# Attention with a woven S5 scan on one core: scores issued behind the second turn of a pair, maxima first on VectorE

## The reference

```python
q, k, v, u = split(h @ w_mix_in)                  # 512 columns each
# attention: 8 heads of 64; for branches (128,1), (512,4), (2048,16)
#   s = q.k * 64**-0.5 - slope_h * distance, masked; softmax; the branches
#   are mixed by their softmax denominators
# S5: 32 groups of 16 channels, 64 complex states each
bu = einsum(u, b_bar); states = scan(a_bar, bu); y = real(einsum(states, c)) + d*u
mixed = concat([attn, ssm]) @ w_mix_out
```

## Time and profile before

| | us |
|---|---|
| median of three runs | 3159.32 |
| lowest, highest | 3157.42, 3162.17 |
| profiled execution | 3157.16 |
| its span | 3155.3 |
| TensorE busy | 3036.2 (96%) |
| VectorE busy | 1376.3 (44%) |
| ScalarE busy | 869.7 (28%) |
| granted TensorE clock, mean | 0.989 |

### The profile page before, as it was taken

One profiled execution on the slowest core, in us unless ns is written; L12 is line 12 of the kernel. 1 busy time (PEld: TensorE's weight loads), 2 busy tenths in 40 slices (PEclk: granted clock), 3 DMA queues, 4 the chain that ended last, 5 costly groups with the idle time before them and its releaser, 6 DMA issues. The chain is left out here.

```text
span 3155.3 us, 36156 instructions
## 1 busy us (share of the span) xinstructions
PE 3036.2 (96%) x13904; PEld 2470.5 (78%) x13904; DVE 1376.3 (44%) x1715; ACT 869.7 (28%) x1313; POOL 411.8 (13%) x1004
## 2 busy tenths in 40 slices
PE   7999999999998989999999999999998999999998
PEld 5767888888886768888888877876677888888886
DVE  5653444444446353433343354335546333333336
ACT  6523211222113252111211133135644211121112
POOL 0001000000000000788870010011100000000000
PEclk9999999999999999999999999999999999999999
DMA  3112111111112022122221132212122111111113
GB/s 125 40 61 80 61 43 44 53 53 53 40 41 67 27 74 67 65 80 87 94 97 40 47 114 87 82 60 71 56 91 105 65 41 47 47 60 47 40 47 127
DMA packets 54405, 206.93 MB, mean 66 GB/s; under 512 B 7216, under 2 KB 7984, under 8 KB 52000
## 3 DMA queue, kind: packets, MB, share of 16 engines
q1 hardware_dynamic: 38592, 140.53, 13.3%
q0 software_dynamic: 15712, 65.02, 5.6%
HBM read 173.15 MB, written 31.20 MB: 65 GB/s over the span
## 5 line engine op out<-in xcount | busy, mean ns | idle before, releaser
L126 PE MATMUL ps<-region_a,region_b 128*128 128x512 f32 x1664 | 658.0, 395 | 18.1 <-DVE region_a L221 9.8
L128 PE MATMUL ps<-region_a,region_b 128*128 128x512 f32 x1664 | 649.9, 391 | 0.0
L127 PE MATMUL ps<-region_a,region_b 128*128 128x512 f32 x1664 | 649.8, 391 | 0.0
L815 DVE TENSOR_TENSOR acc<-acc,ps 128x1024 f32<-128x1024 f32 x288 | 350.9, 1219 | 332.2 <-PE ps L128 332.2
L126 PE MATMUL ps<-region_b,region_a 128*128 128x512 f32 x1088 | 432.6, 398 | 17.3 <-DVE region_b L121 10.0
L127 PE MATMUL ps<-region_b,region_a 128*128 128x512 f32 x1088 | 428.8, 394 | 0.0
L128 PE MATMUL ps<-region_b,region_a 128*128 128x512 f32 x1088 | 428.6, 394 | 0.0
L121 DVE TENSOR_TENSOR region_b<-raw,region_b 128x1024 fp32r<-128x1024 f32 x176 | 218.0, 1254 | 395.3 <-ACT region_b L117 395.1
L126 PEld LDWEIGHTS ps<-region_a,region_b 128*128 128x128 f32 x1664 | 314.2, 189 | 86.3 <-DVE region_b L121 7.3
L128 PEld LDWEIGHTS ps<-region_a,region_b 128*128 128x128 f32 x1664 | 313.7, 189 | 65.8
L127 PEld LDWEIGHTS ps<-region_a,region_b 128*128 128x128 f32 x1664 | 314.2, 189 | 64.8 <-issue 1.7
(11 more groups left out here) (290 smaller groups left out, 3204.5 us busy)
## 6 DMA issues: line engine op xcount, KB each, us to landing
raw<-stream SPq DMA_DIRECT2D x252, 512.0 KB, 3.3
ssm_row<-ssm_mid POOLq DMA_DIRECT2D x8, 1632.0 KB, 7.7
x_mid<-acc POOLq DMA_DIRECT2D x24, 512.0 KB, 3.0
ssm_mid<-made_osc POOLq DMA_DIRECT2D x8, 1024.0 KB, 4.3
ssm_mid<-made_out POOLq DMA_DIRECT2D x8, 608.0 KB, 3.3
acc<-x SPq DMA_DIRECT2D x8, 512.0 KB, 8.2
rold<-x POOLq DMA_DIRECT2D x16, 256.0 KB, 3.4
old_a<-x_mid POOLq DMA_DIRECT2D x8, 512.0 KB, 7.2
```

What stands on the lines that cost most here:

```text
L126: nc.tensor.matmul(psum, lhs(0), rhs(0), start=first, stop=False)
L127: nc.tensor.matmul(psum, lhs(0), rhs(1), start=False, stop=False)
L128: return nc.tensor.matmul(psum, lhs(1), rhs(0), start=False, stop=last)
L815: nc.vector.tensor_tensor(acc[:, t, :], acc[:, t, :], src, ALU.add).then_inc(F.sem["de"], 1)
```

## The change

Three things, in `att_pe` and `att_dve` alone. On TensorE, scores of a pair of blocks go from in front of the turns of the even block n to behind the turns of the odd block n - 1 (`EARLY` holds all odd steps, so it is so for every pair but the one issued at n = 0), and `factors` goes behind the scan's step. On VectorE, the maximum of block n + 2 comes first in each step, then `inverses`, then `finish`. The bias rows for the next pair of heads are made at r = 7 and r = 8, one each, the second behind the finish. What is computed is the same, and no instruction is added or taken away.

```diff
--- before.py
+++ after.py
@@ -1680,7 +1680,8 @@
         ot_hi, ot_lo = sem("ot_hi"), sem("ot_lo")
         NA = N_HEADS * NT
         NQ = NA // 4
-        BIAS_AT = 5
+        BIAS_AT = (7, 8)
+        EARLY = (1, 3, 5, 7)
         TILE_ORDER = (0, 1, 4, 5, 2, 3, 6, 7)
         TURNED_AT = {6: 0, 4: 0, 2: 4 * S, 0: 4 * S}
 
@@ -1808,16 +1809,18 @@
                         ins.then_inc(at_pv, 1)
 
             for n in range(NA):
-                if n % 2 == 0 and n + 2 < NA:
+                if n % 2 == 0 and n + 2 < NA and (n == 0 or (n - 1) % NT not in EARLY):
                     scores_pair(pe, n // 2 + 1)
                 if n == 0:
                     pe.wait_ge(u_out, GT)
                 transposes(n)
-                if n % 4 == 0 and n:
-                    factors(n // 4 - 1)
+                if n % 2 and n + 3 < NA and n % NT in EARLY:
+                    scores_pair(pe, (n + 3) // 2)
                 if n == 0:
                     ssm_turn_pe(pe, 0, 0)
                 ssm_step_pe(pe, n)
+                if n % 4 == 0 and n:
+                    factors(n // 4 - 1)
                 if n >= 4:
                     values(n // 4 - 1, n % 4)
             factors(NQ - 1)
@@ -1876,16 +1879,18 @@
 
             made = {}
             for n in range(NA):
+                if n + 2 < NA:
+                    maximum(dve, n + 2, made.get(block_of(n + 2)[0], 0))
+                if n % 4 == 0 and n:
+                    inverses(n // 4 - 1)
                 if n % 4 == 0 and n >= 8:
                     finish(n // 4 - 2)
-                if n % 4 == 0 and n:
-                    inverses(n // 4 - 1)
-                if n + 2 < NA:
-                    maximum(dve, n + 2, made.get(block_of(n + 2)[0], 0))
-                h, i = block_of(n + 2)
-                if i == BIAS_AT and h + 2 < N_HEADS:
-                    dve.wait_ge(at_m, n + 3)
-                    made[h + 2] = head_bias(dve, h + 2)
+                pair, r = divmod(n, 2 * NT)
+                if r in BIAS_AT and 2 * pair + 2 < N_HEADS:
+                    if pair:
+                        dve.wait_ge(at_m, 2 * NT * pair)
+                    h = 2 * pair + 2 + BIAS_AT.index(r)
+                    made[h] = head_bias(dve, h)
                 ssm_step_dve(dve, n)
                 ssm_rest_dve(dve, n)
             finish(NQ - 2)
```

## The result

The changed kernel takes 3188.15 us (median of 4 runs, 3184.21 to 3191.80) against 3159.59 before (4 runs): ratio 1.0092, 95% interval 1.0079 to 1.0104. It is slower by 28.6 us. Its profiled execution took 3191.8 us, with a span of 3190.0. The two profiled executions differ by 34.6 us in all (3191.8 and 3157.16), so 3.6 us of that lie outside the stage, 3.3 of them behind it, where the order is the same. The part behind the stage took between 864.6 and 868.1 us in the fourteen profiled executions of this document, so I read the 3.6 us as scatter, and the loss as that of the stage that the prediction spoke of.

What follows compares the result with a forecast made beforehand. It took TensorE's queue to be the bound (busy 44.65 of 48.50 us a pair). From 3157.2 us, 23.5 us of waits and 5.5 us of clock gave 3186 us, range 3172 to 3197.

Steps and rivals of the forecast that it cites:

- (a): Bias rows moved to r7 and r8 (blocks r0 to r15 of a pair): 1.65 us wait goes, 0.45 us left.
- (b): At r4 and r12: factor turns newly wait 1.5 us for att_o, the finish being behind maximum and inverses.
- (c): Scores of r8, r9 at r5 newly wait 2.0 us for r7's maximum behind the scan; at r13, 1.6 us.
- (d): Scores at r3 and r11 wait for a maximum queued behind m1b: 0.4 and 0.85 us.
- (e): Turn at r7 waits 0.65 us (before 0.19) for r6's copy, queued on ScalarE; at r15 also 0.65.
- (f): Factor turns at r0 and r8 wait for the finish: 0.25 and 0.1 us (before 0.6 at r0).
- The sum of the waits: TensorE's waits in a new pair, 9.95 against 3.85 us: +6.1 us a pair, +23.5 us over the stage.
- The clock: TensorE's granted clock falls in four surely idle places, 1.1 us each, a little for the rest: +5.5 us.
- 1 (faster): Attention stage: old waits go and new ones do not come, about 2 us a pair won, 3149 us; chance 0.07.
- 2 (even): (c) comes but (b) is hidden, replaced waits pay: 0 to +2 us a pair, 3157 to 3165; chance 0.10.
- 3 (no clock): Attention stage: waits come but gaps are too short for the clock to fall, 3181 us; chance 0.25.
- 4 (a fall in every batch): Clock falls in every batch of the stage at full price, +23.5 + 13, 3194 us; chance 0.2.

Runs made afterwards that it cites:

- The two experiments that cut it, on either engine's side: Against the whole change: scores of r5 and r13 back behind the S5 product, 3173.3 us; add and four scans behind the maximum of r7 and r15, 3171.8 us.
- small filler: The whole change plus unread score products ahead of the scores, two at r5 and one at r13, none in the first pair: 3185.8 us, ratio 1.0091.
- factor turns late: The kernel before, with only the factor turns moved behind the scan's step: 3156.9 us, ratio 0.9992.
- larger filler: The whole change plus unread score products of 512 columns ahead of the scores, three at r5 and two at r13: 3191.8 us, ratio 1.0108.

## Why the prediction was right

The forecast was 3186 us, in a range of 3172 to 3197; measured were 3188.15. That the two lie 2 us apart is in part luck: the forecast puts 29.0 us on the stage, the profiled execution shows 31.0 there and 34.6 in all, and the medians differ by 28.6. The mechanism is what is borne out, pair by pair (us; the last with the end of the stage):

| pair | before | after | longer by | waits forecast | clock low |
|---|---|---|---|---|---|
| 1 | 48.18 | 55.29 | 7.1 | 6.3 | before short, after long |
| 2 | 48.50 | 56.93 | 8.4 | 6.1 | after long |
| 3 | 48.42 | 56.14 | 7.7 | 6.1 | after short |
| 4 | 56.23 | 63.97 | 7.7 | 5 | after long |

The parts, in its order:

- **What bounds the stage**: right. No matmul was added, VectorE's and ScalarE's busy time stayed, and the pair grew by TensorE's waits and clock.
- **(a) bias rows**: right in sign and a little mild in size. The wait of 1.65 us is gone. What is left of the bias row at r8 was walked as 0.45 us; 0.18 us shows ahead of the scores of r9.
- **(b) finish behind maximum and inverses**: 1.5 us forecast at r4 and r12, 1.38 and 1.43 shown. The chain to `att_o` was walked as 2.99 us from the end of the scan product; `att_o` ends at 2158.60 + 0.42 = 2159.02, which is 2.93 behind 2156.09.
- **(c) scores at r5 and r13**: 2.0 and 1.6 us forecast, 1.96 and 1.27 shown. The chain was walked as 6.05 us and is 2162.08 - 2156.09 = 5.99. The two experiments that cut it, on either engine's side, each took 15 to 16 us off, falls of the clock included.
- **(d) scores at r3 and r11**: 0.4 and 0.85 forecast, 0.21 and 0.69 shown. Recorded idle time is shorter than the start-to-start waits that I walked by some 0.15 us, as a matmul's record ends behind its slot; that difference runs through all these pairs of numbers.
- **(e) the turn of r7 and r15**: with the 1.6 us of (c) at r13 the weakest step. 0.65 us forecast; 0.39 shown at r15, and at r7 0.40 in the pair without a fall (the small filler's third), less or nothing where the slow clock fills the wait.
- **(f) factor turns at r0 and r8**: 0.25 forecast, 0.26 shown; at r8 nothing shows.
- **The sum of the waits**: 6.1 us a pair; the pair without a fall of the clock is 54.63 us, 6.2 over 48.42. For the stage 23.5 us forecast, 22.6 to 24.2 by the estimate above.
- **The clock**: right in kind, place and number. Four falls, one at each r5 and none at r13, as "surely idle enough" had it; each costs 1.5 to 2.7 us where 1.1 us was taken, so the term is 6.8 to 8.4 us rather than 5.5. The step that was mis-sized is the price of one fall: the row of before had the low clock for 3.34 us, and in the change a stretch of 6.56 us ran at 0.56. That the fall at the start of the stage would be missing after was not foreseen. By the rule on long single gaps (the Trainium skill, "TensorE: Matmul & The Clock Gate", section "HAM oscillation") the clock would have held. The trace does not agree: the longest gap among the blocks after is 2.04 us, and it fell four times. The measurement decides, and the rows were right to go by.
- **Rivals**: 1 (faster) and 2 (even) fell with the waits of (b) and (c). 3 (no clock) and 4 (a fall in every batch) bracket what happened; four falls in eight batches is the forecast between them. That a waiting matmul lets no other past held: the S5 product had its data at r5 and stood 1.96 us.
- **The signs**: five came as given: the pair of 55 to 57 us, the wait of 1.4 us behind `att_o`, the 1.65 us gone, the bias rows alone, the low clock behind the scores of r8. Two did not: scores behind maxima were to go over 20 us and came to 16.4, since each recorded wait is shorter than walked and (c) at r13 by a fifth; and TensorE's busy time, 44.7 to 46 us in the forecast, is 48.0 and 49.1, by the slow clock and by the same longer records.

The forecast said that 0.2% is what a measurement can tell. That was fair: for kernels run eleven times the interval was about 0.09% to either side (0.13% for the change, run four times), and a gain of 1.6 us in the stage (factor turns late) could not be told from nothing.

## What to carry to other kernels

Moving an instruction earlier in an in-order queue moves its wait earlier too, and uncovers what had stood behind it: before the move, walk the releasing engine's chain from the last event that both engines share, by start-to-start spacings, and compare it with the work left in between. An engine that is 40% idle can still set the time if its work is handed over in one lump; here the cure was to take 2.1 us of work that nobody waited for out of the lump, and not to issue the scores earlier. Waits that one chain sets do not add up: take one away and the next grows, and two edits on one chain have to be measured together.

## What was not expected of the hardware

- A product of 512 columns from one half of the rows, issued one behind another, took 0.86 us in the larger filler (each is recorded as two, and these start 0.43 us apart), while the scores' products, which alternate between the two halves of the rows, take about 0.50 us for each 512 columns (two products of 512 and two of 256, 8 records, in 1.50 us). The records of the scores start in twos, one of each half, 0.01 us apart, and a record of 512 columns took 0.59 us in both cases: the halves ran side by side.
- Whether the clock falls at a place is not settled by the kernel's order alone: with the same filler and the same waits in front of it, it fell in the second pair and held in the third. Where the scores of r5 and r13 were put back it fell nowhere between the start of the stage and the end of the last pair, and where the scans were behind the maximum it fell in the first pair only, behind the gap of 2.04 us.
